# A hybrid decoder step: the feed-forward norm's weights are loaded for each tile, and the row ring has nine places

## The chip, the cores and the metric

One core of a Trainium2 chip runs the whole program. The metric is device time in microseconds for one execution; three executions of the kernel before are shown, and the forecast is for the median of such executions. TensorE is called PE, VectorE DVE, ScalarE ACT, GpSimd POOL and SyncE SP, as in the profile. Sixteen DMA engines serve the core.

## The reference

One layer of a decoder for 1024 new prompt tokens and for 8 sequences with one new token each. Two mixers (latent attention and retention) are merged by gates, and a product-key expert layer follows. What matters here is the second half:

```python
hp = hp + merge_branches(o_lat, o_ret, rg, ga, gb, w_uv[l], ret_norm_g[l], w_oa[l], w_ob[l], w_out[l])
hp = hp + peer(rms_norm(hp, ffn_norm_g[l]), peer_w_q[l], peer_sub_keys[l], peer_u[l], peer_v[l])

def merge_branches(...):
    ...
    return (jax.nn.sigmoid(ga) * o_a + jax.nn.sigmoid(gb) * o_b) @ w_out

def peer(xn, w_q, sub_keys, expert_u, expert_v):
    ...
    act = jax.nn.gelu(jnp.einsum('thkd,td->thk', expert_u[eid], tb))
    return jnp.einsum('thk,thkd->td', g * act, expert_v[eid])
```

In `peer`, `tb` is a block of 128 tokens, and `eid` and `g` are the numbers and gates of its 8 x 16 chosen experts per token. `ffn_norm_g` is one vector of 1024 floats; `rms_norm` scales each token's row by its own root mean square and multiplies by that vector. Each token reads 128 rows of `expert_u` and 128 of `expert_v`, 4 KB each.

## The kernel before

**Tiles.** The prompt is 8 tiles of 128 tokens (t = 0 to 7); the 8 new tokens are a ninth tile (t = T = 8, "sample"). For each tile a *front* computes everything up to the chosen experts: projections, retention, attention, merge, output projection, feed-forward norm, the expert queries and the two rounds of top-16. Then the *experts* of the tile are worked through, 128 pairs of a `u` row and a `v` row per token. `beside(front, experts, pairs)` deals 64 double steps of the experts of tile t-1 in between the steps of the front of tile t, on each of PE, DVE and ACT alike, so that both advance in an order written into the program. Only the front of tile 0 has no experts beside it.

**The experts.** POOL does nothing but gathers: one indirect DMA brings one row for each of 128 tokens, 128 x 4 KB, into a place of `rows`. The list `turns` gives their order: 20 `u` rows first (LAG), then `u` and `v` in turn. Gather i goes to place i % RING, and `wait_row_free` makes POOL wait until the gather RING turns earlier has been used. A `u` row is used by a dot product with `px` on DVE (L1912); a `v` row is scaled and summed either on PE through a diagonal matrix (L1053) or on DVE (L1938). The first `u` gather of a tile waits also for the tile's chosen numbers (`chosen`, DVE L1720, tile `pe_id`).

**The weight stream.** SP loads all matrices in blocks, in the order in which PE uses them, as chunks of 0.5 MB into the four places of `wbuf`. Chunk n waits until PE has used chunk n-4 (`w_used`). For each tile the end of the order is `oa`, `gate`, `out` (two blocks of four chunks), `wq`. DMAs that SP issues go down SP's own hardware queue (q1 in the profile) in the order of issue; the gathers are in the software queue q0.

**Around the change.** DVE forms the gated sum in L1614 to L1616 and signals `merged`; PE transposes it (`mT`) and then multiplies by the `out` blocks; DVE adds the result to the residual (L1627), takes the sum of squares (L1630), and L1634 writes `xn2` from the residual, the row scale and `ffn_gain`, and signals `x2_normed`. `ffn_gain` is a buffer of its own, 128 partitions x 1024 floats, loaded once at the start by one of ACT's 13 constant loads. The work buffer `WK` is four stretches of 1024 floats that are reused through a front; its second stretch, `WK[:, D:2*D]`, is read last by L1615 before the merge and written next by ACT with the expert queries, after `x2_normed`. In the sample tile it also holds `p_pad`, which `dve_sample_lists` clears.

Of the kernel before, what the change touches and what calls it, by code (L numbers as in the profile page):

```python
# [13 lines left out]
ALU = mybir.AluOpType  # L14
# [7 lines left out]
P = 128  # L22
# [73 lines left out]
def program(nc, a, out, const):  # L96
    _, SEQ, D = a["x_prompt"].shape
# [12 lines left out]
    T = SEQ // P  # L110
# [5 lines left out]
    O_RV = O_RQ + 2 * RH * RDK  # L116
    O_RG = O_RV + RH * RDV
    O_GA = O_RG + RH * RDV
    RING = 8


    w_in, w_uq, w_oa, w_ob, w_out, w_q = (a[n][0] for n in ("w_in", "w_uq", "w_oa", "w_ob", "w_out", "peer_w_q"))
# [28 lines left out]
    with ExitStack() as ctx:  # L151
        def sb(name, words, dt=F32):
            return ctx.enter_context(nc.sbuf_tensor(name, [P, words], dt))

        def sem(name):
            return ctx.enter_context(nc.semaphore(name))

        def signal(name, per=1):
            return Signal(sem(name), per)
# [3 lines left out]


        ident = sb("ident", P)
        ffn_gain = sb("ffn_gain", D)
        final_gain = sb("final_gain", D)
        kv_gain = sb("kv_gain", KVL)
        attn_gain_t = sb("attn_gain_t", KC)
# [19 lines left out]

        rows = sb("rows", RING * D)  # L190
        wbuf = sb("wbuf", WSLOTS * KPS * BW)
# [12 lines left out]
        WK = sb("WK", max(4 * D, NPAGES * P) + 8)  # L204
        sc = [WK[:, 0:D], WK[:, 3 * D:4 * D]]
        pt = WK[:, D:2 * D]
        maskb = WK[:, 2 * D:3 * D]
        xn2 = maskb
        xload = WK[:, 3 * D:4 * D]
        oa = WK[:, 3 * D:4 * D]  # L210
        rqk = WK[:, 3 * D:4 * D]
# [122 lines left out]
        merged = signal("merged")  # L334
        x2_normed = signal("x2_normed")
# [6 lines left out]
        ckv_stored = sem("ckv_stored")  # L342
        fd = Link(sem("front_steps"))
        pdl = Link(sem("expert_steps"))
        gate_pool, gate_dve, gate_pe, gate_sp = (sem(f"{e}_passed") for e in ("pool", "dve", "pe", "sp"))
        row_in = [sem(f"row_arrived{i}") for i in range(RING)]
        u_used = signal("u_used", P)

# [22 lines left out]
        def row_slot(kind, n):  # L371
            i = turn_of[kind, n] % RING
            return rows[:, i * D:(i + 1) * D]

        def wait_row(eng, kind, n):
            i = turn_of[kind, n]
            eng.wait_ge(row_in[i % RING], 16 * (i // RING + 1))

        def wait_row_free(eng, i):
            if i < RING:  # L380
                return
            kind, n = turns[i - RING]
            if kind == "u":
                eng.wait_ge(u_used.sem, n + 1)
            elif on_pe[n]:
                eng.wait_ge(v_pe_used.sem, pe_before[n + 1])
            else:
                eng.wait_ge(v_dve_used.sem, dve_before[n + 1])
# [66 lines left out]
        def sp_blocks(sp, t, name):  # L455
            for i in range(count[name]):
                n0, k = load_at[t, name, i]
                for n in range(n0, n0 + k):
                    _, _, w, k0, kn, c, wd = loads[n]
                    if n >= WSLOTS:  # L460
                        sp.wait_ge(w_used, n + 1 - WSLOTS)
                    at = (n % WSLOTS) * KPS * BW
                    sp.dma_start(wbuf[:, at:at + kn * wd].rearrange("p (k c) -> p k c", k=kn),
                                 w[k0 * P:(k0 + kn) * P, c:c + wd].rearrange("(k p) c -> p k c", p=P)
                                 ).then_inc(w_in_s[n % WSLOTS], 16)

        def sp_rope(sp, t):
            q_roped.wait(sp, t - 1)
            sp.dma_start(ropeb[:, :], const["rope"][ds(t * P, P), :]).then_inc(rope_in.sem, 16)
# [590 lines left out]
        def _(pe):  # L1060
            pe.wait_ge(first_in, 32)
            for _ in pe_linA(pe, 0):
                pass
            pe.wait_ge(const_in, 16 * CONST_LOADS)
            pe.wait_ge(setup_in, 16)
# [356 lines left out]
        V = nc.vector  # L1422

        def rsqrt(dve, link, x, n, tmp):

            y, u = tmp[:, 0:n], tmp[:, n:2 * n]
            link(dve, V.tensor_scalar(y.bitcast(I32), x.bitcast(I32), -0.5, RSQRT_MAGIC, ALU.mult, ALU.add))
            for _ in range(3):
                link(dve, V.scalar_tensor_tensor(out=u, in0=y, scalar=-0.5, in1=y, op0=ALU.mult, op1=ALU.mult))
                link(dve, V.tensor_tensor(u, u, x, ALU.mult))  # L1430
                link(dve, V.scalar_tensor_tensor(out=y, in0=u, scalar=1.5, in1=y, op0=ALU.add, op1=ALU.mult))
            return y
# [47 lines left out]
        def dve_front(dve, t, sample=False):  # L1480
# [3 lines left out]
            xin = xr[t % 2]  # L1484
# [3 lines left out]
                                             op0=ALU.mult, op1=ALU.add, accum_out=stat[:, 1:2]))  # L1488
            link(dve, V.tensor_tensor_reduce(out=knat[:, 0:KVL], in0=z[:, O_CKV:O_KR], in1=z[:, O_CKV:O_KR], scale=1.0,
                                             scalar=0.0, op0=ALU.mult, op1=ALU.add, accum_out=stat[:, 2:3]))  # L1490
            link.mark(V.tensor_scalar(stat[:, 1:2], stat[:, 1:2], 1.0 / QL, EPS, ALU.mult, ALU.add))
            link(dve, V.tensor_scalar(stat[:, 2:3], stat[:, 2:3], 1.0 / KVL, EPS, ALU.mult, ALU.add))
            r = rsqrt(dve, link, stat[:, 1:3], 2, nr)
            link.mark(V.tensor_scalar(z[:, 0:QL], z[:, 0:QL], r[:, 0:1], None, ALU.mult))
            V.scalar_tensor_tensor(out=z[:, O_CKV:O_KR], in0=z[:, O_CKV:O_KR], scalar=r[:, 1:2], in1=kv_gain[:, :],
                                   op0=ALU.mult, op1=ALU.mult).then_inc(lat_normed.sem, 1)
# [45 lines left out]
            else:  # L1542
# [14 lines left out]
                for h in range(RH):  # L1557
                    hs = slice(h * RDV, (h + 1) * RDV)
                    ins = V.scalar_tensor_tensor(out=state[:, hs], in0=state[:, hs], scalar=const["chunk_decay"][h],
                                                 in1=DD.bank(tj, "stateU")[:, hs], op0=ALU.mult, op1=ALU.add)  # L1560
# [57 lines left out]
            for i in range(2):  # L1618
# [6 lines left out]
                else:  # L1625
# [5 lines left out]
                                             op1=ALU.add, accum_out=stat[:, 3:4]))  # L1631
            link(dve, V.tensor_scalar(stat[:, 3:4], stat[:, 3:4], 1.0 / D, EPS, ALU.mult, ALU.add))
            r = rsqrt(dve, link, stat[:, 3:4], 1, nr)
            V.scalar_tensor_tensor(out=xn2, in0=xin[:, :], scalar=r, in1=ffn_gain[:, :], op0=ALU.mult,  # L1634
                                   op1=ALU.mult).then_inc(x2_normed.sem, 1)
            yield "x2"

# [31 lines left out]
            r = rsqrt(dve, link, ssq[:, :], 2 * PH, nr)  # L1669
# [59 lines left out]
        def dve_sample_lists(dve):  # L1729
            link = fd  # L1730
            n, lists = PH * NB, slice(0, PH * NB)
            V.memset(p_pad, 0.0).then_inc(p_built, 1)
            V.memset(p_one, 1.0).then_inc(p_built, 1)
            V.tensor_copy(p_owner.rearrange("p (k b) -> p k b", b=NB),
# [5 lines left out]
            r = rsqrt(dve, link, ssq[:, :], 2 * PH, nr)  # L1740
# [282 lines left out]
        @block.scalar  # L2023
        def _(act):
            n = 0
            for dst, src in ((decay_t[:, :], const["decay"]), (q_decay[:, :], const["q_decay"]),
                             (k_decay[:, :], const["k_decay"]), (iota16[:, :], const["iota16"]), (diag8[:, :], const["diag8"]),
                             (ret_eye[:, :], const["ret_eye"]),
                             (ffn_gain[:, :], a["ffn_norm_g"].broadcast_to([P, D])),
                             (final_gain[:, :], a["final_norm_g"].rearrange("(a d) -> a d", a=1).broadcast_to([P, D])),  # L2030
                             (kv_gain[:, :], a["kv_norm_g"].broadcast_to([P, KVL])),
                             (uk[:, :].rearrange("p (k c) -> p k c", k=2), a["w_uk"][0].rearrange("(k p) h n -> p k (h n)", p=P)),
                             (uv[:, :].rearrange("p (k c) -> p k c", k=2), a["w_uv"][0].rearrange("(k p) h n -> p k (h n)", p=P)),
                             ):
                act.dma_start(dst, src).then_inc(const_in, 16)
                n += 16
            with nc.allow_non_contiguous_dma("gains are read once, one value per partition"):
                for dst, src in ((q_gain_t, a["q_norm_g"]), (ret_gain_t, a["ret_norm_g"])):
                    act.dma_start(dst[:, :], src[0].rearrange("(k p) -> p k", p=P)).then_inc(const_in, 16)
                    n += 16  # L2040
            assert n == CONST_LOADS * 16
            act.dma_start(rows[:, 0:2 * PH * PD].rearrange("p (g d) -> p g d", g=2 * PH),
                         a["peer_sub_keys"][0].rearrange("s h k d -> k (s h) d")).then_inc(setup_in, 16)
            act.dma_start(pages_reg[0:1, :], a["page_table"].rearrange("(o b) n -> o (b n)", o=1)).then_inc(table_in, 16)
            act.wait_ge(first_in, 32)
            for _ in act_linA(act, 0):
                pass
            act.wait_ge(const_in, 16 * CONST_LOADS)
            for i in range(4):
                KJ.wait_filled(act, 0, "keys", i)  # L2050
                nc.scalar.activation(keys_t[:, 4 * i * P:4 * (i + 1) * P], KJ.bank(0, "keys", i), ACT.Copy).then_inc(KJ.drained, 1)
            experts = act_experts(act)
            beside(act_front(act, 0), experts, 0)
            for t in range(1, T):
                beside(act_front(act, t), experts, NPAIR // 2)
            beside(act_front(act, T, sample=True), experts, (NPAIR + LAG) // 2, SAMPLE_SHARES)
            act.wait_ge(p_spread, 2)
            nc.scalar.activation(p_x[:, :], PS[:, 512:3 * 512], ACT.Copy).then_inc(p_rows_out, 1)
            act.wait_ge(p_gelu_in, 1)
            nc.scalar.activation(p_gb, p_ga, ACT.Tanh, scale=GELU_C).then_inc(p_tanh, 1)  # L2060

        @block.vector
        def _(dve):
            dve_x_norm(dve, 0)
            dve.wait_ge(const_in, 16 * CONST_LOADS)
            dve.wait_ge(first_in, 32)
# [25 lines left out]
PAGE_SLOTS = 16  # L2092
CORNER = ((0, 1, 16, 0), (1, 3, 8, 16), (4, 4, 4, 40), (8, 8, 1, 56))
NCAND = 64
CONST_LOADS = 13
VECTOR_TURNS = ((0, 7), (47, 51), (63, 64))
LAG = 20

# [67 lines left out]
```

## Time and profile before

| what | value |
|---|---|
| runs (3) | 4265.44, 4285.19, 4293.67 us; median 4285.19 us |
| span of the profiled execution | 4263.9 us |
| PE busy | 3286.0 us (77%) |
| DVE busy | 2707.6 us (64%) |
| POOL busy | 2504.8 us (59%), gathers |
| DMA moved | 1547.20 MB, mean 363 GB/s |
| gathers (software queue) | 1082.26 MB, 65.9% of 16 engines' span |
| SP's queue | 450.78 MB, 29.4% |

The span is the time from the first to the last instruction of one execution under the profiler; no other time of that execution is given, and the three runs were timed apart from it. The span lies within 2 us of the fastest of the three runs and 21 us (0.5%) under their median. Shares are averages: the DMA engines are busy nearly throughout, while each compute engine has free time.

### The profile page before, as it was taken

The numbers are of one execution on the slowest core, as the hardware profiler recorded it, in microseconds if no ns is written. First come the engines' busy times: TensorE is split into PE (matmuls) and PEld (weight loads), VectorE is DVE, ScalarE is ACT, GpSimd is POOL, SyncE is SP. The second block draws the span as 40 slices with busy tenths as digits, with TensorE's granted clock in tenths as the row PEclk, the third lists the DMA queues.
The fourth block names the chain that finished last, engine by engine and source line by source line (L and its number), as shares of the span: only waits on it lengthen the run. The fifth ranks groups of instructions, "written<-read, shape, count | busy, mean of one in ns | idle before, by whom it ended". The sixth has DMA issues, their size and how long they took to land.

```text
span 4263.9 us, 45831 instructions
## 1 busy us (share of the span) xinstructions
PE 3286.0 (77%) x14597; PEld 1588.9 (37%) x14597; DVE 2707.6 (64%) x6168; ACT 695.2 (16%) x2141; POOL 2504.8 (59%) x2069
## 2 busy tenths in 40 slices
PE   7877777877787777877788777877787767799754
PEld 3333333433343233433343334433343323466422
DVE  2157568655776577656876677757775686666534
ACT  2112111211121011211121112201121111111111
POOL 0007667666666666776766666766767575445442
PEclk9988999998999999999999999999999986899877
DMA  5669999999999999999999999999999999999895
GB/s 191 212 222 353 403 394 379 378 392 401 392 366 399 402 384 380 383 401 402 385 373 403 402 391 368 393 402 394 379 380 399 396 390 343 322 343 353 295 380 192
DMA packets 606562, 1547.20 MB, mean 363 GB/s; under 512 B 92114, under 2 KB 149083, under 8 KB 606323
## 3 DMA queue, kind: packets, MB, share of 16 engines
q0 software_dynamic: 297216, 1082.26, 65.9%
q1 hardware_dynamic: 272018, 450.78, 29.4%
q10 hardware_dynamic: 37090, 11.24, 1.1%
q8 instruction: 118, 1.93, 0.2%
q14 instruction: 120, 0.98, 0.1%
HBM read 1533.93 MB, written 10.13 MB: 362 GB/s over the span
## 4 chain that ended last, share of the span: by engine, by line
PE 39%; DMA 32%; POOL 9%; DVE 8%; issue 6%; ACT 4%; ACTq 1%; POOLq 0%; DVEq 0%; SPq 0%
DMA rows<-in_peer_v_dram,pe_id 21%; PE PS L1053 15%; PE PS L704 13%; POOL rows L622 9%; DMA rows<-in_peer_u_dram,pe_id 6%; PE PS L970 3%; DMA wbuf<-in_w_in_dram 2%; DVE rows L1912 2%; PE PS L682 1%; DMA wbuf<-in_w_out_dram 1%; DMA wbuf<-in_peer_w_q_dram 1%; PE PS L808 1%; PE PS L828 1%; ACT diags L2018 1%; PE PS L745 1%
## 5 line engine op out<-in xcount | busy, mean ns | idle before, releaser
L1053 PE MATMUL PS<-rows,diags 128*128 128x512 f32 x2496 | 1371.0, 681 | 625.9 <-DMA rows<-in_peer_v_dram,pe_id 422.9
L622 POOL DMA_INDIRECT rows<-in_peer_u_dram,pe_id x1024 | 1228.7, 1200 | 934.2 <-DVE dots L1912 368.9
L622 POOL DMA_INDIRECT rows<-in_peer_v_dram,pe_id x1024 | 1256.9, 1227 | 763.0 <-PE PS L1053 506.7
L1912 DVE CUSTOM_DVE_ANT_0 rows<-rows,px 128x1024 f32<-128x1024 f32 x1024 | 1245.3, 1223 | 646.9 <-DMA rows<-in_peer_u_dram,pe_id 642.8
L704 PE MATMUL PS<-wbuf,xt 128*128 128x512 f32 (+1 forms) x2048 | 927.8, 596 | 55.9 <-DMA wbuf<-in_w_in_dram 41.5
L1053 PEld LDWEIGHTS PS<-rows,diags 128*128 128x128 f32 x2496 | 480.2, 209 | 1279.7 <-issue 923.9
L704 PEld LDWEIGHTS PS<-wbuf,xt 128*128 128x128 f32 x2048 | 398.8, 200 | 574.8 <-issue 454.5
L1938 DVE SCALAR_TENSOR_TENSOR xr<-rows,gcoef,xr 128x1024 f32<-128x1024 f32 x400 | 513.2, 1283 | 154.2 <-issue 138.6
L704 PE MATMUL PS<-wbuf,wide 128*128 128x512 f32 (+1 forms) x736 | 338.7, 602 | 32.0 <-ACT wide L1121 14.4
L2018 ACT ACTIVATE diags<-ident,gcoef 128x128 f32<-128x128 f32 x624 | 222.0, 397 | 85.8 <-issue 40.9
L704 PEld LDWEIGHTS PS<-wbuf,wide 128*128 128x128 f32 x736 | 143.9, 200 | 211.0 <-issue 164.5
L1110 ACT ACTIVATE z<-PS 128x512 f32<-128x512 f32 x80 | 43.7, 567 | 669.8 <-PE PS L704 669.8
L682 PE MATMUL PS<-ident,WK 128*128 128x128 f32 x572 | 94.6, 308 | 58.2 <-DVE WK L1634 25.6
L682 PEld LDWEIGHTS PS<-ident,WK 128*128 128x128 f32 x572 | 77.8, 159 | 110.0 <-DVE WK L1634 36.6
L1110 ACT ACTIVATE WK<-PS 128x512 f32<-128x512 f32 x48 | 28.7, 597 | 489.6 <-PE PS L704 489.6
L828 PE MATMUL PS<-KV,WK 128*128 128x64 f32 x576 | 81.9, 290 | 29.9 <-ACT WK L1238 29.8
L808 PE MATMUL PS<-KV,qt 96*128 96x512 f32 (+3 forms) x192 | 78.3, 518 | 28.1 <-DVE mx L1586 26.5
L828 PEld LDWEIGHTS PS<-KV,WK 128*128 128x128 f32 x576 | 73.1, 200 | 46.3 <-ACT WK L1238 40.6
L1586 DVE CUSTOM_DVE_ANT_0 WK<-PS,WK 128x128 f32<-128x128 f32 (+7 forms) x64 | 48.2, 753 | 58.8 <-PE PS L808 58.8
L1912 DVE DVE_READ_ACCUMULATOR2_ANT dots<- 128x1 f32 x1024 | 83.3, 81 | 0.0
L1233 ACT ACTIVATE WK<-WK,nmx 128x128 f32<-128x128 f32 (+7 forms) x64 | 49.5, 774 | 205.0 <-DVE nmx L1590 204.9
L1627 DVE TENSOR_TENSOR xr<-PS,xr 128x512 f32<-128x512 f32 x16 | 11.1, 691 | 105.0 <-PE PS L704 105.0
(347 smaller groups left out, 2458.0 us busy)
## 6 DMA issues: line engine op xcount, KB each, us to landing
wbuf<-in_w_in_dram SPq DMA_DIRECT2D x396, 512.0 KB
wbuf<-in_peer_w_q_dram SPq DMA_DIRECT2D x144, 512.0 KB
wbuf<-in_w_ob_dram SPq DMA_DIRECT2D x72, 512.0 KB
wbuf<-in_w_out_dram SPq DMA_DIRECT2D x72, 512.0 KB
wbuf<-in_w_oa_dram SPq DMA_DIRECT2D x36, 512.0 KB
rows<-in_peer_u_dram,pe_id POOLq DMA_INDIRECT x1028, 5.9
rows<-in_peer_v_dram,pe_id POOLq DMA_INDIRECT x1024
KV<-in_cache_ckv_dram SPq DMA_DIRECT2D x128, 128.0 KB
```

The lines of the kernel that those rows point to most:

```text
L622: pool.indirect_dma_start(row_slot(kind, n), None, a["peer_u" if kind == "u" else "peer_v"][0], bass.IndirectOffsetOnAxis(ap=pe_id[t % 2][ ...
L682: last = nc.tensor.transpose(b[0:m, k * n:(k + 1) * n], src, ident[0:n, 0:n])
L704: last = nc.tensor.matmul(bnk, lhs[:, (k0 + j) * P:(k0 + j + 1) * P], wbuf[:, at + j * wd:at + (j + 1) * wd], start=(k0 + j == 0), stop=(n ...
L808: last = nc.tensor.matmul(DD.bank(tj, "score", h)[:, i:i + w], qt[0:HD, h * P:(h + 1) * P], key_t[0:HD, h, i:i + w], start=True, stop=True)
L828: last = nc.tensor.matmul(bank[6][:, h * VH:(h + 1) * VH], pt[:, k * P:(k + 1) * P], value[:, k, h * VH:(h + 1) * VH], start=(k == 0), sto ...
L970: last = nc.tensor.matmul(PS[quarter, at_:at_ + P], qsc[b % 2][quarter, k * 32:(k + 1) * 32], blocks_of[quarter, k] if k < 8 else turned[c ...
L1053: last = nc.tensor.matmul(bank[3 + 4 * c], diag(n), row_slot("v", n)[:, c * 512:(c + 1) * 512], start=start, stop=stop)
L1110: return nc.scalar.activation(dst[:, at_:at_ + wd], b[:, 0:wd], func, scale=scale)
L1233: nc.scalar.activation(sc[h % 2][:, 0:w], sc[h % 2][:, 0:w], ACT.Exp, bias=nmx[:, h:h + 1], scale=SCALE, accum_out=sums[:, h:h + 1]).then_ ...
L1912: V.tensor_tensor_reduce(out=row, in0=row, in1=px[:, :], scale=1.0, scalar=0.0, op0=ALU.mult, op1=ALU.add, accum_out=dots[:, at_:at_ + 1]) ...
L1938: V.scalar_tensor_tensor(out=y[:, :], in0=row_slot("v", n), scalar=gcoef[:, g % 2 * TOPK + k:g % 2 * TOPK + k + 1], in1=y[:, :], op0=ALU.m ...
L2018: nc.scalar.activation(diag(n), ident[:, :], ACT.Copy, scale=gcoef[:, g % 2 * TOPK + k:g % 2 * TOPK + k + 1]).then_inc(diag_ready.sem, 1)
```

## The change

The own buffer `ffn_gain` goes. Its name now stands for the second stretch of `WK`, and SP loads it anew for each of the nine tiles, between the two `out` blocks, after a wait for `merged`; the load is 0.5 MB, the vector repeated over the 128 partitions. DVE waits for it ahead of L1634. The freed 4 KB per partition go to `rows`, whose ring has nine places where it had eight. ACT's constant loads are 12. In the sample tile DVE waits for `x2_normed` before it clears `p_pad`, which lies in the same stretch. The line with four unused semaphores goes out in exchange for the new one.

```diff
-    RING = 8
+    RING = 9
...
-        ffn_gain = sb("ffn_gain", D)
...
         xn2 = maskb
+        ffn_gain = WK[:, D:2 * D]
...
-        gate_pool, gate_dve, gate_pe, gate_sp = (sem(f"{e}_passed") for e in ("pool", "dve", "pe", "sp"))
+        gain_in = signal("gain_in", 16)
...
                                  ).then_inc(w_in_s[n % WSLOTS], 16)
+                if name == "out" and i == 0:
+                    merged.wait(sp, t)
+                    sp.dma_start(ffn_gain, a["ffn_norm_g"].broadcast_to([P, D])).then_inc(gain_in.sem, 16)
...
             r = rsqrt(dve, link, stat[:, 3:4], 1, nr)
-            V.scalar_tensor_tensor(out=xn2, in0=xin[:, :], scalar=r, in1=ffn_gain[:, :], op0=ALU.mult,
+            gain_in.wait(dve, t)
+            V.scalar_tensor_tensor(out=xn2, in0=xin[:, :], scalar=r, in1=ffn_gain, op0=ALU.mult,
                                    op1=ALU.mult).then_inc(x2_normed.sem, 1)
...
             n, lists = PH * NB, slice(0, PH * NB)
+            x2_normed.wait(dve, T)
             V.memset(p_pad, 0.0).then_inc(p_built, 1)
...
-                             (ffn_gain[:, :], a["ffn_norm_g"].broadcast_to([P, D])),
...
-CONST_LOADS = 13
+CONST_LOADS = 12
```

SP's order of issue in the first tile, from the `oa` blocks on; `in_w_in` here are the four `gate` blocks, and a number after x counts chunks. Before:

```order
L463 DMA wbuf<-in_w_oa_dram 128x2x512 [waits w_used] x4
L463 DMA wbuf<-in_w_in_dram 128x2x512 [waits w_used] x16
L463 DMA wbuf<-in_w_out_dram 128x2x512 [waits w_used] x8
L463 DMA wbuf<-in_peer_w_q_dram 128x2x512 [waits w_used] x16
L469 DMA ropeb<-const_rope_dram 128x240 [waits q_roped]
```

And now:

```order
L463 DMA wbuf<-in_w_oa_dram 128x2x512 [waits w_used] x4
L463 DMA wbuf<-in_w_in_dram 128x2x512 [waits w_used] x16
L463 DMA wbuf<-in_w_out_dram 128x2x512 [waits w_used] x4
L468 DMA WK<-in_ffn_norm_g_dram 128x1024 [waits merged]
L463 DMA wbuf<-in_w_out_dram 128x2x512 [waits w_used] x4
L463 DMA wbuf<-in_peer_w_q_dram 128x2x512 [waits w_used] x16
L472 DMA ropeb<-const_rope_dram 128x240 [waits q_roped]
```

The load and its wait stand between the fourth and the fifth chunk of `out`, ahead of the sixteen chunks of the expert queries.

POOL's gathers in the steady part, where `u` and `v` alternate; the name after "waits" is the signal that frees the place. Before:

```order
L622 DMA rows<-in_peer_v_dram,pe_id0 128x1024 [waits v_dve_used]
L622 DMA rows<-in_peer_u_dram,pe_id0 128x1024 [waits u_used]
L622 DMA rows<-in_peer_v_dram,pe_id0 128x1024 [waits v_pe_used]
L622 DMA rows<-in_peer_u_dram,pe_id0 128x1024 [waits u_used]
L622 DMA rows<-in_peer_v_dram,pe_id0 128x1024 [waits v_dve_used]
```

And now:

```order
L625 DMA rows<-in_peer_v_dram,pe_id0 128x1024 [waits u_used]
L625 DMA rows<-in_peer_u_dram,pe_id0 128x1024 [waits v_dve_used]
L625 DMA rows<-in_peer_v_dram,pe_id0 128x1024 [waits u_used]
L625 DMA rows<-in_peer_u_dram,pe_id0 128x1024 [waits v_pe_used]
L625 DMA rows<-in_peer_v_dram,pe_id0 128x1024 [waits u_used]
```

No gather has moved in POOL's order. With an odd number of places a `u` gather takes the place of a `v` row and the other way round, and each waits for the use that lies nine turns back in place of eight.

## Rows read from the trace of the kernel before

**Rows 1.** The page: busy time, and the DMA lines of its 40 slices.
```profile
PE 3286.0 (77%) x14597; PEld 1588.9 (37%) x14597; DVE 2707.6 (64%) x6168; ACT 695.2 (16%) x2141; POOL 2504.8 (59%) x2069
...
DMA  5669999999999999999999999999999999999895
GB/s 191 212 222 353 403 394 379 378 392 401 392 366 399 402 384 380 383 401 402 385 373 403 402 391 368 393 402 394 379 380 399 396 390 343 322 343 353 295 380 192
```

**Rows 2.** Windows of the span: busy us (instructions) of each engine, PEclk, DMA share, GB/s.
```profile
core 0: us, PE busy (x) PEld busy (x) DVE busy (x) ACT busy (x) POOL busy (x), PEclk, DMA share, GB/s
350.00:3450.00 3100.00, 2422.16 (x6419) 1117.12 (x6420) 2119.71 (x4762) 515.29 (x1548) 2091.68 (x1715) 0.93 1.01 390
...
3650.00:4000.00 350.00, 322.09 (x5530) 208.88 (x5529) 216.58 (x403) 53.97 (x164) 172.43 (x152) 0.96 0.99 333
4000.00:4264.00 264.00, 143.65 (x1273) 68.20 (x1273) 108.21 (x234) 40.72 (x166) 92.75 (x80) 0.73 0.78 288
...
749.00:1213.00 464.00, 359.01 (x896) 162.97 (x894) 314.99 (x714) 73.17 (x226) 308.77 (x257) 0.92 1.01 389
...
950.00:1000.00 50.00, 33.96 (x74) 13.44 (x75) 28.87 (x41) 5.87 (x16) 36.19 (x25) 0.93 1.03 402
```

**Rows 3.** DMA view of one tile's period, 749 to 1213 us, in 40 slices.
```profile
GB/s 347 403 403 394 360 351 409 361 378 404 399 350 408 384 379 401 401 402 401 400 402 406 399 402 405 392 403 401 402 399 404 351 363 403 400 402 402 403 324 345
DMA packets 61576, 180.28 MB, mean 389 GB/s; under 512 B 5746, under 2 KB 7538, under 8 KB 61558
```

**Rows 4.** Waits of POOL, 749 to 1213 us: total, times, longest.
```profile
POOL rows L622 <- issue: 68.4, 206, 4.2
POOL rows L622 <- PE PS L1053: 63.3, 40, 3.9
POOL rows L622 <- DVE dots L1912: 23.8, 11, 5.6
```

**Rows 5.** Chain of waits in order of time: start us, us, what.
```profile
499.63 13.64 DMA rows<-in_peer_v_dram,pe_id
...
4128.68 13.95 DMA wbuf<-in_w_out_dram
```

**Rows 6.** Timeline of POOL at a tile's end: start us, us.
```profile
727.23 0.97 POOL L622 DMA_INDIRECT rows<-in_peer_v_dram,pe_id  x1 [1.90 <-PE PS L1053]
731.25 1.74 POOL L622 DMA_INDIRECT rows<-in_peer_u_dram,pe_id  x1 [3.04 <-DVE dots L1912]
733.29 3.05 POOL L622 DMA_INDIRECT rows<-in_peer_v_dram,pe_id  x1 [0.30 <-issue]
...
744.96 0.93 POOL L622 DMA_INDIRECT rows<-in_peer_u_dram,pe_id  x1 [0.30 <-issue]
```

**Rows 7.** Timeline of DVE in the same stretch.
```profile
733.24 2.29 DVE L1716 TENSOR_TENSOR WK<-WK,sif 128x2048 f32<-128x2048 f32 x1
...
741.72 0.23 DVE L1720 CAST pe_id<-i 128x128 uint32<-128x128 f32 x1
```

**Rows 8.** Timeline around the merge of a tile: DVE, PE, SP.
```profile
522.86 1.22 DVE L1616 TENSOR_TENSOR WK<-WK,wide 128x1024 f32<-128x1024 f32 x1
...
524.14 1.09 PE L682 MATMUL PS<-ident,WK 128*128 128x128 f32 x8 [1.19 <-DVE WK L1616]
532.55 2.65 PE L704 MATMUL PS<-wbuf,wide 128*128 128x512 f32 x4
...
535.24 7.23 SPq L463 DMA_DIRECT2D wbuf<-in_w_out_dram  x4
...
563.32 1.28 DVE L1634 SCALAR_TENSOR_TENSOR WK<-xr,nr,ffn_gain 128x1024 f32<-128x1024 f32 x1
```

**Rows 9.** SP's DMA queue, 510 to 529 us, then 530 to 536 us: packets, MB, share.
```profile
q1 hardware_dynamic: 1321, 2.56, 35.7%
...
q1 hardware_dynamic: 1, 0.00, 0.0%
```

**Rows 10.** DMA issues: KB each, median us to landing.
```profile
ffn_gain<-in_ffn_norm_g_dram ACTq DMA_DIRECT2D x1, 512.0 KB, 8.0
```

## The prediction

> **What bounds the kernel now.** I read the page's busy times first, then its slices, then one tile's period, and last the waits of the engine that feeds the DMA engines. No compute engine is full: PE is busy for 77% of the span, DVE 64%, POOL 59%, while the DMA engines stand at 9 tenths in 35 of 40 slices [rows 1]. From 350 to 3450 us, where the experts of one tile run beside the front of the next, the DMA share is 1.01 and 390 GB/s move; in an undisturbed stretch it is 1.03 and 402 GB/s [rows 2]. The 40 slices of one period (464 us) make it plain: more than half stand at 399 to 409 GB/s and a dozen fall to 324 to 384 [rows 3]. So most of the time the DMA engines are the bound, at about 402 GB/s, and in short dips they are not fed. The period moves 180.28 MB; at 402 GB/s this is 448.5 us, and 15.5 of the 464 us are lost in dips. The DMA share tells how much of that is idleness and not slow packets: 1.03 less 1.01 of 464 us is 9.3 us.
>
> Why are they not fed? POOL spends 308.8 us of the period on 257 gathers and 68.4 us on the gaps of 0.3 us between them, and waits for free places for 63.3 us (a `v` row in use on PE) and 23.8 us (a `u` row in use on DVE) [rows 2, 4]. So POOL has 87 us to spare, and the ring holds it back. In a full stretch that wait costs nothing: a gather issued at 499.63 lands 13.64 us later [rows 5], since eight gathers of 0.524 MB and weights are queued ahead of the bytes. At a tile's end it does cost: DVE is deep in the list work of the front, a `u` row's dot comes late, POOL stands for 3.04 us, and the gather after the next takes 3.05 us while DVE runs L1716 for 2.29 us; a gather with DVE out of the way takes 0.93 us [rows 6, 7]. The slices at this place of the period are 324, 345 and 347 GB/s, the deepest dip [rows 3].
>
> **The ninth place.** It lets one more gather be under way or landed when the users fall behind. Where the engines are full it gives nothing: the bytes are the same and only the wait in the queue grows, by 1.3 us. In a dip it is worth at most the DMA time of one gather, 0.524 MB at 402 GB/s = 1.30 us, once for each passage from "all places under way" to "all places landed", since the place has to be filled anew between two dips. The dips of the period, in slices of 11.6 us [rows 3], each slice's loss being (402 - rate)/402 x 11.6 us: the tile's end with the start of the next (324, 345, 347) 5.5 us; slices 5 to 9 (360, 351, 361, 378) 4.6; slices 12 to 15 (350, 384, 379) 2.7; slices 32 and 33 (351, 363) 2.6. By the share above 0.6 of each is idleness, so every one of the four still holds more than 1.30 us. Bounds: nothing, and 6 x 1.30 = 7.8 us a tile if the two longer groups in the middle are two dips each. The nearest rows are the four groups, 5.2 us. I take three of them, 3.9 us: at the tile's end DVE itself has no free time and POOL's gathers are stretched by it [rows 6, 7], so there I count on nothing. Seven tiles run beside experts: 27 us, with 0 and 55 us as ends. In the sample part from 3650 us on PE is busy for 322 of 350 us at 333 GB/s, and after 4000 us the DMA share is 0.78 [rows 2]; one or two dips there are worth 1.3 to 2.6 us.
>
> What is late next? The first `u` gather of a tile needs `pe_id`. It is written by 741.95, and POOL reached that gather at 744.96 (the 237th in its list), after two slow ones [rows 6, 7]. Nine places bring POOL there earlier by one gather, 1.2 to 2.0 us with its gap, so the 3.0 us of slack hold with about 1 us to spare.
>
> **The nine loads.** Each moves 0.524 MB, so 1.30 us of full DMA engines. Seven fall into full periods: 9.1 us. Tile 0's lies before the gathers begin and takes the place of the one dropped at the start, in a stretch at 191 to 222 GB/s [rows 1]: nothing. The sample tile's follows `merged` there, where the chain runs through the `out` chunks (13.95 us to land) [rows 5]; taken at 1.3 us, which cancels the dips of that part. Bounds of one load: 0, if it falls into a dip, and below nothing it can't go, since the bytes are new; the dear end is the next paragraph's. The constant load that goes had landed after 8.0 us [rows 10], far ahead of any use.
>
> **The wait in SP's queue.** SP now waits for `merged` ahead of the load. Behind it stand `out` chunks 5 to 8 and the `wq` chunks. Chunk 5 waits anyway until PE has used chunk 1, and that follows `merged`: L1616 ends at 524.08, PE transposes at 524.14 and begins on `out` at 532.55 [rows 8]. So the wait holds up nothing. The load then stands behind the chunks issued before it. SP's queue moved 2.56 MB from 510 to 529 us, 135 GB/s beside the gathers, and nothing from 530 to 536 us [rows 9]: chunk 4 was through by then, and chunk 5 was issued at 535.24 [rows 8]. The load fills that gap: 0.524 MB at 135 GB/s is 3.9 us, to about 534 us, with 1 to 2 us in hand. What it takes there it takes from the gathers, the 1.30 us above. L1634, which needs the load, starts 39 us after `merged` [rows 8]: DVE doesn't wait. In the sample tile the wait for `x2_normed` is for DVE's own last instruction, 1.28 us, once: under 2 us in sum.
>
> Sum against the profiled execution: 4263.9 - 27 + 9 = 4246 us of span, and 18 us off the median, 4285.2 - 18 = **4267 us**.
>
> The Trainium skill (DMA: Bandwidth & Descriptors, Where 436 GB/s comes from) says that HBM gives a core about 358 GB/s and binds there. By that the mean of 363 GB/s would already be the ceiling, there would be no dips to fill, and only the new bytes would count, some 12 us more. The trace speaks against it, with whole stretches at 401 to 403 GB/s, and it is part of the first rival's chance only.
>
> **Rivals.**
> (1) *The place gives nothing and the bytes cost.* What fails in a dip is POOL's issuing, not its places: with gathers of 0.93 + 0.3 us its best pace is 1.23 us [rows 6] against the DMA engines' 1.30, and DVE's long operations stretch single gathers to 1.7 to 3 us. Or nine gathers can't be under way at once. Against it: 87 us of waiting for places in each period [rows 4]. Price: +9 to +12 us, 4295 us. The Trainium skill (SBUF — State Buffer, Who interferes with whom) has a rule for this: a DVE instruction with two SBUF inputs contends with a GpSimd instruction that reads SBUF; rows 6 and 7 agree, with 3.05 against 0.93 us.
> (2) *Slower: the load stands before chunk 5.* If it is still in SP's queue when PE has used chunk 1, chunks 5 to 8 land later and PE waits in the middle of `out`, with the experts behind it in PE's order. It decides once the load is through later than 535 us on the clock of rows 8; with the whole 3.9 us of it ahead of chunk 5 in each of eight tiles, and the idle PE eating what the ring gives, 9 + 31 = 40 us, 4325 us. For it: the margin is only 1 to 2 us, and a queue of nine gathers slows the weights too, which take 13.95 us to land in places [rows 5]. Against it: the gap is there, and PE, busy for 359 of the period's 464 us [rows 2], has waits in which a chunk that is 1 or 2 us late costs nothing.
> (3) *All dips go.* If each dip is the last part of a stall just longer than eight places, and the engines stay ahead once they are, most of the 9.3 us of idleness and part of the slow packets go: 12 us a tile, 84 less 9: 75 off, 4210 us. Against it: POOL's pace of 1.23 us refills a place hardly faster than it is emptied.
>
> **How the numbers follow.** Forecast 0.62 (its own range, from the ring's ends of 55 and 5 us: 4240 to 4290); rival 1 0.20; rival 2 0.06; rival 3 0.07; the change not doing what it says (the places never used) is inside rival 1; the rest, 0.05, is spread. From 4238 to 4298 us both the forecast and rival 1 lie inside, with rivals 2 and 3 out. One per cent of 4285 is 43 us, about what a measurement of this kernel can tell from no change: faster than 4242 takes rival 3 and the edge of the forecast, 0.13; slower than 4328 takes the dear half of rival 2 and a part of the rest, 0.06; between them 0.81.
>
> **What would show it.** In the profile after: the period between two copies into `px` down from 464 to about 461 us; slices at 402 GB/s unchanged and the middle dips shallower, with the tile's end as before; POOL's waits for places below 87 us; a gather landing after 15 us in full stretches; one load of 0.5 MB for each tile right behind `merged`, and no wait of DVE for it; 4 MB more moved. I am wrong if POOL begins to wait for `pe_id` at every tile, if PE waits for `out` chunks, or if the dips turn out to be set by DVE alone.

## The result, and the profile after

| | kernel before | changed kernel |
|---|---|---|
| median of the runs | 4280.87 us (5 runs, 4265.44 to 4293.67) | 4235.78 us (5 runs, 4226.87 to 4249.49) |
| span of the profiled execution | 4263.9 us | 4235.1 us |

The ratio is 0.9899, 95% interval 0.9877 to 0.9921: 43 us or 1.0% faster, where 18 us were forecast and 4238 us was the low end of the range. The profiled execution of before was itself near the fast end of its runs, so these two spans show only 29 us; for the comparison of traces below both kernels ran once more on one chip.

The page of the changed kernel: busy times, DMA share, rate, packets and bytes, and SP's queue.

```profile
PE 3267.6 (77%) x14597; PEld 1581.6 (37%) x14597; DVE 2704.7 (64%) x6168; ACT 696.4 (16%) x2141; POOL 2505.0 (59%) x2069
...
DMA  5668999999999999999999999999999999999895
GB/s 187 217 228 333 403 390 393 386 400 399 398 384 398 402 390 389 390 403 400 390 385 403 393 397 382 398 402 398 386 383 399 398 396 339 339 344 350 309 387 183
DMA packets 607714, 1551.40 MB, mean 366 GB/s; under 512 B 92242, under 2 KB 149211, under 8 KB 607475
...
q1 hardware_dynamic: 273314, 455.50, 29.8%
```

4.2 MB more are moved than before (1551.40 against 1547.20), which are the eight loads that are new on balance, and PE and DVE do what they did. The window from 350 to 3450 us, which answers to [rows 2], then one tile's period as in [rows 3], then POOL's waits in the same 3100 us:

```profile
350.00:3450.00 3100.00, 2423.44 (x6525) 1118.33 (x6526) 2135.09 (x4823) 519.96 (x1557) 2100.30 (x1726) 0.93 1.02 394
```

```profile
GB/s 350 386 405 405 410 359 372 408 397 405 409 375 399 406 395 403 400 402 400 401 401 404 404 400 403 376 404 401 401 400 403 406 373 397 402 401 402 402 398 340
DMA packets 61775, 181.00 MB, mean 395 GB/s; under 512 B 5771, under 2 KB 7563, under 8 KB 61756
```

```profile
POOL rows L625 <- issue: 428.1, 1369, 3.7
POOL rows L625 <- PE PS L1056: 393.7, 267, 4.5
POOL rows L625 <- DVE dots L1917: 174.4, 85, 4.4
```

The rate in the window is 394 GB/s where it was 390, at a DMA share of 1.02 for 1.01. The full stretches stand at 400 to 406 GB/s as before; the dips are fewer and shallower. The period is 458 us long where it was 464. POOL waits for places almost as long as before (393.7 + 174.4 us; 412.1 + 164.7 us in the same window of before; in the period shown 80 us where 87 were): most of that waiting is in full stretches, where it costs nothing, and it is a poor measure of the gain.

The nine loads: SP's issue of them with the time to landing, and the surroundings of the second one, in the stretch of [rows 8].

```profile
L468 SPq DMA_DIRECT2D WK<-in_ffn_norm_g_dram x9: 340/340/346, 188.6 to 4103.6; - x9
DMA to landing us min/median/max: 3.3/8.9/11.6
```

```profile
525.23 1.25 DVE L1619 TENSOR_TENSOR WK<-WK,wide 128x1024 f32<-128x1024 f32 x1
...
526.51 0.34 SPq L468 DMA_DIRECT2D WK<-in_ffn_norm_g_dram  x1
...
537.26 7.52 SPq L463 DMA_DIRECT2D wbuf<-in_w_out_dram  x4
```

SP issues the load 0.03 us after L1619 (the old L1616) ends, at 526.48, and chunk 5 of `out` at 537.26. The nine loads land 3.3 to 11.6 us after their issue, this one 10.7 us, and L1638 (the old L1634) never waits for it: its group shows no idle time in front of it. The end of a tile's lists, on POOL and DVE:

```profile
1201.86 0.94 POOL L625 DMA_INDIRECT rows<-in_peer_v_dram,pe_id  x1 [0.30 <-issue]
1203.11 1.77 POOL L625 DMA_INDIRECT rows<-in_peer_u_dram,pe_id  x1 [0.30 <-issue]
...
1201.95 0.23 DVE L1724 CAST pe_id<-i 128x128 uint32<-128x128 f32 x1
```

The gather at 1203.11 is the 237th in POOL's list, the new tile's first `u` row; `pe_id` is complete at 1202.18, 0.9 us earlier.

### The profile page after: what moved, and what is told of

The parts are those of the page before. It is cut to its first block, busy times and chain, and to the rows that moved or that the text cites. A ratio compares the mean times of both kernels' runs of the same rounds, so it can differ in the third digit from the quotient of the medians.

```text
span 4235.1 us, 45848 instructions
## 1 busy us (share of the span) xinstructions
PE 3267.6 (77%) x14597; PEld 1581.6 (37%) x14597; DVE 2704.7 (64%) x6168; ACT 696.4 (16%) x2141; POOL 2505.0 (59%) x2069
## 2 busy tenths in 40 slices
DMA packets 607714, 1551.40 MB, mean 366 GB/s; under 512 B 92242, under 2 KB 149211, under 8 KB 607475
## 4 chain that ended last, share of the span: by engine, by line
PE 38%; DMA 28%; DVE 12%; POOL 10%; issue 6%; ACT 4%; ACTq 1%; SPq 0%; POOLq 0%; DVEq 0%
DMA rows<-in_peer_v_dram,pe_id 16%; PE PS L1056 14%; PE PS L707 13%; POOL rows L625 10%; DMA rows<-in_peer_u_dram,pe_id 5%; DMA wbuf<-in_w_in_dram 3%; DVE rows L1917 3%; PE PS L973 3%; DMA wbuf<-in_w_out_dram 2%; PE PS L685 2%; DMA wbuf<-in_peer_w_q_dram 1%; PE PS L811 1%; PE PS L831 1%; DVE xr L1943 1%; PE PS L748 1%
## 5 line engine op out<-in xcount | busy, mean ns | idle before, releaser
L625 POOL DMA_INDIRECT rows<-in_peer_u_dram,pe_id x1024 | 1263.4, 1234 | 995.4 <-PE PS L1056 442.4
L625 POOL DMA_INDIRECT rows<-in_peer_v_dram,pe_id x1024 | 1222.4, 1194 | 659.5 <-DVE dots L1917 348.2
L1464 DVE MAX8 sv<-wide 128x8 f32<-128x128 f32 x129 | 28.1, 280 | 90.7 <-ACT wide L1284 89.1
```

Of the source, the lines that this page charges most:

```text
L625: pool.indirect_dma_start(row_slot(kind, n), None, a["peer_u" if kind == "u" else "peer_v"][0], bass.IndirectOffsetOnAxis(ap=pe_id[t % 2][ ...
```

## The experiments

Each row is a ratio to the kernel before, run on the same chip, with its 95% interval. "Load" is the load for each tile.

| run | places | load | other | ratio |
|---|---|---|---|---|
| b0_before_again | 8 | no | | 0.9991 (0.9981 to 1.0002) |
| a0_after_again | 9 | yes | | 0.9893 (0.9878 to 0.9908) |
| a1_after_third | 9 | yes | | 0.9902 (0.9882 to 0.9922) |
| e1_ring9_no_load | 9 | no | | 0.9884 (0.9857 to 0.9910) |
| e2_ring8_load | 8 | yes | | 1.0024 (1.0007 to 1.0041) |
| g2_ring8_again | 8 | yes | | 1.0039 (1.0025 to 1.0054) |
| e3_ring9_wait8 | 9 | yes | waits of eight | 1.0034 (1.0017 to 1.0051) |
| e4_ring10 | 10 | yes | | 0.9889 (0.9861 to 0.9916) |
| e9_ring10_again | 10 | yes | | 0.9894 (0.9871 to 0.9916) |
| e5_ring7 | 7 | yes | | 1.0272 (1.0251 to 1.0293) |
| e6_load_twice | 9 | two | | 0.9912 (0.9897 to 0.9928) |
| e7_pe_later | 9 | yes | only the wait for `v` rows later | 1.0018 (1.0004 to 1.0032) |
| e8_dve_later | 9 | yes | only the wait for dots later | 1.0095 (1.0075 to 1.0115) |
| f3_second_wait | 9 | yes | idle second wait | 0.9884 (0.9866 to 0.9902) |
| f1_short9 | 9 | yes | short lists | 0.9862 (0.9846 to 0.9879) |
| f2_short8 | 8 | yes | short lists | 0.9968 (0.9953 to 0.9983) |

The sets ran on different chips. In two of them every kernel took some 150 us longer, the kernel before 4428 and 4435 us in place of 4281, nearly all of it beside the sample front; so times are compared only within a set, by ratios.

### Is it the place, and what does the load cost?

e1, nine places without the load:

```diff
-        ffn_gain = WK[:, D:2 * D]
+        ffn_gain = final_gain[:, :]
...
-                if name == "out" and i == 0:
-                    merged.wait(sp, t)
-                    sp.dma_start(ffn_gain, a["ffn_norm_g"].broadcast_to([P, D])).then_inc(gain_in.sem, 16)
...
-            gain_in.wait(dve, t)
```

> Nine places, and no load for each tile: the final norm's weights, which are resident, are read in the place of the feed-forward norm's (this part of the computation is changed, so other experts are chosen; the number of gathers is the same). If each load costs its DMA time (1.3 us in seven full periods, 9 us in all), this run is 9 us faster than the changed kernel, about 4227 us. If the loads fall into free DMA time and cost nothing, it is equal to it, 4236 us. The period between the first u gathers of two tiles goes from 458 us to 457 us by the first theory and stays by the second.

e2 and, on another chip, g2: the changed kernel with `RING = 8`.

> Eight places and the load for each tile. If the place is the whole gain and the load costs 1.3 us a tile, this is slower than the kernel before by 9 us, about 4290 us. If the load costs nothing, 4281 us. A rival, that the gain comes from something else in the edit than the ring, would show as a time below 4270 us.

> Eight places and the load, full list work, on the same chip as the others of this set: 1.0024.

e6, a second load behind the first:

```diff
+                    sp.dma_start(z[:, D:2 * D], a["ffn_norm_g"].broadcast_to([P, D])).then_inc(gain_in.sem, 16)
...
-        gain_in = signal("gain_in", 16)
+        gain_in = signal("gain_in", 32)
```

> Nine places and a second load of the same 0.5 MB right behind the first, into a part of z that is free there, with DVE waiting for both. If the load's price is its bytes (1.3 us each), 9 to 12 us above the changed kernel, ratio +0.0025. If the first load fills a gap in SP's queue of 1 to 2 us more than its own length, the second one stands before chunk 5 of out and PE waits: up to 3.9 us a tile, 30 us, ratio +0.007.

The load alone makes the kernel slower by 0.24% and 0.39% (10 and 17 us). A second load costs 0.19% (0.9912 against 0.9893, 8 us), and leaving it out saves 0.1 to 0.2% (e1, 0.9884, against 0.9893, 0.9899 and 0.9902 of the changed kernel on other chips). Each of these differences has an uncertainty of 0.15 to 0.3%, and together they stand around the 9 us that bytes over 402 GB/s give. That the load makes PE wait longer for chunks of `out` is refuted. The main group of its waits for them over the whole execution (total, times, longest), first in the changed kernel (a0), then in the kernel before (b0):

```profile
PE PS L707 <- DMA wbuf<-in_w_out_dram: 7.4, 8, 1.6
```

```profile
PE PS L704 <- DMA wbuf<-in_w_out_dram: 9.1, 6, 1.7
```

With the smaller groups (L703 and L700) these waits are 10.8 us in a0 and 11.5 us in b0, and with the second load of e6 3.7 us.

The ninth place is worth the rest of the difference: 1.0024 or 1.0039 down to 0.9893 or 0.9902, 1.2 to 1.5%, 52 to 63 us. On one chip alone, g2 (1.0039) against f3 below (nine places and an idle second wait, 0.9884), it is 1.55%, 66 us.

### Depth, or the odd number?

e3 has nine places in memory and the waits of eight:

```diff
-            if i < RING:
+            if i < 8:
                 return
-            kind, n = turns[i - RING]
+            kind, n = turns[i - 8]
```

> Nine places in memory, but POOL waits for the use that lies eight turns back, so at most eight are taken. If depth is what helps, the time is that of eight places with the load, 4281 to 4290 us. If the odd number of places helps in itself (u and v rows change places, other addresses), it stays at 4236 us.

It came out like eight places with the load, 1.0034. So other addresses and the exchange of places between `u` and `v` rows bring nothing; being able to run one gather further ahead does.

### Both kernels on one chip, and other depths

> The kernel before, unchanged, to have its trace from the same chip as the others of this set: ratio 1.000. Its period between the first u gathers of two tiles stands against that of the run with nine places.

> The changed kernel, unchanged, on the same chip: ratio 0.990 if the first comparison holds on another chip. If the gain of the place is the whole effect and a load costs what it cost with eight places (0.24%), the place alone is worth 1.2 to 1.3%, about 55 us, and nine places without the load (0.988 in the first set) lie 0.002 below this run. If the load is free with nine places, this run is at 0.988 too.

Here the spans are 4289.5 and 4229.6 us, 60 us apart. The starts of the 237th gather and of every 256th behind it cut the span into tiles: 748.4 to 3539.0 us for six periods of the kernel before, 465.1 us each; 741.7 to 3490.8 us, 458.2 us each, with nine places. That is 41.5 of the 60 us; the period before them gives 4.8, the last, beside the sample front, 11.8 (598.8 down to 587.0 us); the start up to the first gather differs by 1.9, and the tail is 151.7 and 151.8 us. The granted clock of PE is the same in both: 0.93 from 350 to 3450 us, 0.87 beside the sample front.

Not all of the 60 us is the change: b0's profiled execution took 14 us more than the median of its ten runs (4291.27 against 4276.89 us), a0's was within 1 us of its median. Two other pairs give the spread. In the traces of the first comparison six periods are 463.2 and 459.0 us in the mean, 4.2 us apart, and the part beside the sample front 593.3 and 585.0 us. On one chip, with the load in both, eight places (g2) and nine (f3) have 467.5 and 460.1 us, 7.4 us apart, and 592.2 and 585.5 us.

One period, first of the kernel before, then of the changed one, each in 40 slices:

```profile
GB/s 334 404 403 407 396 303 379 404 347 406 410 400 407 405 403 402 401 401 401 400 402 406 401 400 406 376 401 400 402 399 405 385 327 405 403 401 402 401 395 306
DMA packets 61656, 180.59 MB, mean 391 GB/s; under 512 B 5752, under 2 KB 7544, under 8 KB 61637
```

```profile
GB/s 334 402 404 406 409 370 400 407 397 406 396 404 408 403 402 401 402 401 402 401 401 407 402 401 404 381 402 402 401 399 402 408 354 404 402 401 403 401 398 323
DMA packets 61697, 180.73 MB, mean 396 GB/s; under 512 B 5758, under 2 KB 7550, under 8 KB 61678
```

The losses against 402 GB/s, worked out as in the prediction. Tile's end and start (306 and 334, with the 395; then 323, 334 and 398): 4.9 and 4.3 us. Slices 5 to 9 (396, 303, 379, 347; then 370, 397): 5.3 and 1.1 us. Slices 32 and 33 (385, 327; then 354): 2.6 and 1.4 us. The place has taken 0.6 us from the first, 4.2 from the second and 1.3 from the third. Single periods differ a good deal (slices 6 and 9 fall to 264 and 234 GB/s in others of b0, and to 305 and 349 in others of a0), but the means of all six periods, in slices 39 to 2, 4 to 10 and 31 to 34, are close: 0.7, 4.3 and 1.1 us between b0 and a0, and 1.2, 3.2 and 1.5 us between g2 and f3. A gather in a full stretch now takes 15.3 us to land, by the chain of waits of the changed kernel:

```profile
969.67 15.28 DMA rows<-in_peer_v_dram,pe_id
```

Seven places (`RING = 7`) and ten. For ten the buffer of the final norm's weights is given up:

```diff
-    RING = 9
+    RING = 10
...
-        final_gain = sb("final_gain", D)
...
-            V.scalar_tensor_tensor(out=y[0:n, :], in0=y[0:n, :], scalar=r, in1=final_gain[0:n, :], op0=ALU.mult,
+            V.scalar_tensor_tensor(out=y[0:n, :], in0=y[0:n, :], scalar=r, in1=px[0:n, :], op0=ALU.mult,
```

> Seven places and the load. If each place is worth the same at every dip, this is as far above eight places with the load (1.0024) as nine are below it: 1.015. If the worth of a place falls with the number of places (ten gave no more than nine), it is further: 1.02 or over. If the odd number itself helps, it is below 1.01.

> Ten places; the buffer of the final norm's weights is given up for it, and the final norm multiplies by the normed row of the next tile instead (the outputs y are not the reference's). If each place is worth up to 1.3 us per dip, and the dips after the change still hold about two thirds of the idle time of before, ten places give a further 15 to 25 us: about 4215 us. Against it stands the wait for pe_id: POOL reaches the first u gather of a tile only 1.0 us after pe_id is written with nine places, and one gather earlier is 1.2 to 2.0 us, so POOL begins to wait there and the dip at the tile's end gains little: 4222 to 4230 us. If nine places had already taken all there is, 4236 us.

> Ten places as before (the final norm multiplies by the normed row of the next tile, so y is not the reference's), on one chip with nine places. Seven to eight places gave 2.5%, eight to nine 1.3%. If the worth of a place halves each time, ten are 0.6% under nine, 25 us. If the first set holds (0.9889 against 0.9893 to 0.9899), they are within 0.2%.

> The changed kernel on the same chip as the three above: 0.9895.

From seven to eight places the gain is 2.3 to 2.5% (1.0272 to 1.0024 or 1.0039), from eight to nine 1.2 to 1.5%, from nine to ten, on one chip, 0.08% with an uncertainty of 0.3%. One period of seven places:

```profile
GB/s 367 401 366 352 321 340 400 355 375 372 385 406 406 405 403 401 402 400 403 400 402 406 395 403 331 337 403 401 402 400 403 327 333 406 402 403 401 401 371 292
DMA packets 61778, 181.03 MB, mean 382 GB/s; under 512 B 5765, under 2 KB 7557, under 8 KB 61760
```

Not only are the dips deeper; two of them are four slices long (366, 352, 321, 340 and 355, 375, 372, 385). The losses come to 24 us of the period, against 13.6 with eight places and 7.5 with nine. As the mean of six periods, each one's length less its bytes at 402 GB/s, they are 27, 16 and 8 us (e5, b0 and a0, one chip). And one period of nine and then of ten places (a1 and e9), from one chip:

```profile
GB/s 338 399 404 406 410 318 364 408 343 408 406 403 406 404 403 401 402 401 401 402 401 403 405 401 402 369 405 402 401 400 402 408 377 403 403 402 400 402 398 322
DMA packets 61726, 180.91 MB, mean 393 GB/s; under 512 B 5762, under 2 KB 7426, under 8 KB 61707
```

```profile
GB/s 355 392 404 405 411 322 363 407 407 402 408 403 406 403 404 401 402 401 402 402 402 405 403 402 401 407 402 401 402 398 403 408 400 402 401 402 402 401 398 306
DMA packets 61759, 181.01 MB, mean 396 GB/s; under 512 B 5769, under 2 KB 7433, under 8 KB 61740
```

The tenth place has closed what nine had left in single slices (343, 369 and 377 go to 407, 407 and 400), but the two deep dips stay as they are: 318 and 364 GB/s against 322 and 363, and the tile's end 322 and 338 against 306 and 355. The six periods are 461.4 and 459.9 us in the mean. POOL's wait for `pe_id` is not what stops the tenth place; it is 0.9 us, once, in e4's window from 350 to 3450 us.

### Which of the two waits?

e7 gives the `u` gathers a second wait, for the use eight turns back; e8 gives it to the `v` gathers. f3 is the control, with a second wait that has always passed.

```diff
                 wait_row_free(pool, i)
+                if kind == "u":
+                    wait_row_free(pool, i, 8)
```

(e8: `kind == "v"`; f3: `kind == "v"` and 12 in place of 8.)

> Nine places and the load; a u gather waits both for the dot eight turns back and for the v row nine turns back, so only the wait for PE's (or DVE's) use of a v row moves one turn later than with eight places. In the profile before, POOL waits 63 us a period for v rows in use and 24 us for u rows. If the gain goes with these waits, this run keeps most of it: about 0.993, between 1.0024 with eight places and 0.9895 with nine. If it comes from riding over DVE's long operations, which hold up the dots, it keeps little: 1.000.

> The counterpart: a v gather waits for the v row eight turns back and for the dot eight turns back, a u gather for the v row nine turns back, so only the wait for the dot moves one turn later. If the gain is with the v rows, this run has little of it: 0.999. If it is with the dots, most: 0.992. If both waits have to move before a place helps, both runs stay near 1.0024.

> Nine places and the load; each v gather has a second wait, for the use twelve turns back, which has always happened. It gives the price of a second wait on a gather, which the two runs with one wait moved have and the plain kernels haven't. If it costs nothing: 0.990. If it costs 0.1 us or so on POOL for 1024 gathers, and that is felt: up to 100 us, 1.01, and then the two runs say nothing of which wait matters.

A second wait costs nothing that can be seen (0.9884). Then e7, against the three runs with eight turns (1.0024 to 1.0039), says that moving only the wait for `v` rows brings 0.1 to 0.2%, which is within the uncertainty of such a difference, and e8 that moving only the wait for the dots brings less than nothing. The waits only change sides: from 350 to 3450 us POOL waits 571.5 us for dots in e7, where it is 171.8 us in e2. The place has to serve both kinds, or it isn't worth having. Why e8 is slower by 0.6 to 0.7% than eight places, though it waits for no use earlier than they do, no run here shows. Its trace has one mark: POOL waits 117.2 us for `v` rows that DVE scales (L1945), where it is 3.4 us in e2. The reason stays open.

### DVE's long operations at a tile's end

f1 (nine places) and f2 (eight) leave out the six one-hot operations of 2.3 us, with the small ones between them, and make the expert numbers from the lists directly:

```diff
-                link(dve, V.tensor_tensor(oh.rearrange("p (s a) -> p s a", s=P), spread(tf[:, :], P, TOPK),
-                                          over(edges[:, :], P, TOPK), op))
...
-            link(dve, V.scalar_tensor_tensor(out=i0[:, :], in0=i0[:, :], scalar=float(NK), in1=i1[:, :], op0=ALU.mult, op1=ALU.add))
+            link(dve, V.scalar_tensor_tensor(out=i0[:, :], in0=sif[:, 0:P], scalar=float(NK), in1=sif[:, P:2 * P], op0=ALU.mult, op1=ALU.add))
```

> Nine places and the load, with a front whose last list work is left out: the position lists are not turned into key numbers by the six one-hot operations of 128x2048 (L1713, L1716, L1718 and their first round, 2.3 us each); the expert numbers are made from the k-th best keys of the two halves instead, so other experts are chosen (as many gathers). With its counterpart of eight places it tells whether the dips that a place fills come from DVE's long operations at a tile's end: about 14 us of DVE's work a tile go.

> The same with eight places. If a place is worth what it is because of the dip at the tile's end alone, eight and nine places differ by under 0.5% here, where they differ by 1.25% with the full list work. If the place is worth something at every dip of the period, as many small ones, they still differ by about 1%. Against eight places with the full list work this run gains the tile's-end dip, 5 us a tile, 35 us: 0.994.

Without that work the ninth place is still worth 1.06% (0.9968 to 0.9862), 45 us, against 1.2 to 1.5% with it, or 1.55% on the same chip. So between a tenth and a third of its worth goes with that work, and most of it lies elsewhere. In the mean of six periods the loss at the tile's end falls from 4.8 to 1.7 us with eight places (g2, f2) and from 3.6 to 0.3 us with nine (f3, f1): the place is worth 1.2 us there with the work and 1.4 us without. The work itself costs 0.7%, 30 us, with eight places (g2 and f2; 35 us were expected), and 0.2 to 0.3% with nine (f3 and f1, same chip; a0 and f1). The window from 350 to 3450 us of f1 has 396 GB/s at share 1.02; f2's has 390:

```profile
350.00:3450.00 3100.00, 2431.81 (x6598) 1121.38 (x6599) 2049.82 (x4754) 520.29 (x1563) 2083.52 (x1735) 0.93 1.02 396
```

```profile
350.00:3450.00 3100.00, 2424.15 (x6422) 1120.99 (x6422) 2029.25 (x4674) 518.66 (x1552) 2066.89 (x1712) 0.93 1.02 390
```

## Why the prediction was wrong, point by point

- **The bound** was read rightly: DMA engines full at 402 GB/s between dips, and full stretches unchanged in all runs, while nine, eight and seven places differ only in the dips. The about 358 GB/s of the Trainium skill (DMA: Bandwidth & Descriptors, Where 436 GB/s comes from) aren't the ceiling of this kernel: whole periods move 396 GB/s. The Trainium skill works the figure out there as one of two equal shares of an HBM stack; this program uses one core, and no run here shows a core beside a busy neighbour.
- **The ninth place: this step failed, by its size.** It said that a place is worth "at most the DMA time of one gather, once for each passage", counted four groups of dips in a period and took three, 3.9 us a tile and 27 us in all. Measured are 7.4 us a tile as the mean of six periods with the load in both kernels (g2 and f3), 6.1 us slice by slice in one period of b0 and a0, and 52 to 66 us in all, where the upper ends were put at 7.8 and 55 us. The cap of 1.30 us holds about for the dip in slices 32 and 33 (1.1 to 1.5 us in the means). It fails for slices 5 to 9, which were taken as one dip and gave 4.2 us, more than three times the cap (3.2 and 4.3 us in the means): a slice of 11.6 us doesn't separate the stalls in it, and that there are several, with the ring refilled between them, is argued from the size and not shown. From seven to eight places the mean period falls from 477.7 to 467.5 us (e5 and g2, two chips), 10.2 us, more than six dips times 1.30 us allow. The tile's end, counted at nothing, gave 0.6 us in that period, and 0.7 and 1.2 us in the means: little, but it is a part of what is missing.
- **The part beside the sample front** was set at 1.3 to 2.6 us and cancelled against a load. It gave 11.8 us between b0 and a0, and 8.3 and 6.7 us in the other two pairs. The step rested on PE being busy for 322 of 350 us in it and overlooked that POOL waits there too, for DVE's dots, 185.5 us from 3550 to 4100 us in b0 and 172.1 in a0; that this is why is argued, not shown.
- **The load's price**, 9 us: the four measurements, from 4 to 17 us, stand around it. Its place in SP's queue was right as well. It fills the gap between chunk 4 and chunk 5 with less in hand than the 1 to 2 us said (10.7 us to landing after an issue at 526.51, chunk 5 issued at 537.26), and even a second load there costs only its bytes, so rival 2 is refuted.
- **The next wait**, `pe_id`, was right: 0.9 us of slack where about 1 us was said. With ten places it isn't felt either.
- **Rival 1** is refuted by e3 against the changed kernel. POOL's issuing isn't the limit in most dips. **Rival 3** was 75 us off, too far: 8 us of loss remain in a period of a0, in the mean. The truth lies between the forecast and rival 3, a little beyond the far end of the forecast's own range.
- **The median and the span.** The sum was made against a span of 4263.9 us, and the three runs of before had a median 4 us above that of the later five; neither explains the miss.

## What to carry to other kernels

Where a ring of buffers feeds saturated DMA engines, don't price a further place by counting visible dips times one transfer: a dip in the view can be several stalls, and here the eighth and the ninth place each removed about half of the remaining loss (27, 16, 8 us of a period with seven, eight, nine), and the tenth little more. The slope is best had from the other side: one run with a place fewer tells on which part of the curve the kernel is. A constant that is needed once for each tile can live in memory that is free at that time, if its load has a gap in its queue; it costs its bytes.

## What the runs showed of the hardware

A second semaphore wait on each of 1024 gathers had no measurable price (0.9884 against 0.9893 to 0.9902 without). A load that repeats one 4 KB row over 128 partitions costs about what 0.5 MB costs beside gathers: 8 us for nine more of them, with an uncertainty as large, where their bytes at 402 GB/s are 12 us. And sets on different chips differ in one part of a kernel alone: in two of them the part beside the sample front took about 140 us longer (726 against 587 us from the 1773rd gather to the 2029th, same kernel), while the tile periods were within 1% of the others. What makes that part longer there, no run shows.
